# A causal depthwise convolution as Toeplitz products: from two token phases of 64 channels to four token phases of 32 channels

## The chip, the cores and the metric

The kernel runs on one core of one Trainium2 chip. The metric is the device time of one execution in microseconds (us). The engines are named PE (TensorE, matmul), PEld (its weight loads), DVE (VectorE), ACT (ScalarE), POOL (GpSimd) and SP (SyncE, which issues the weight DMAs).

## The reference, cut to what matters

The program is a transformer of two blocks over 512 tokens with 1024 channels, all in float32. The change touches one piece of the first block, the convolution branch of the hybrid mixer:

```python
proj = xn @ w_in                    # 1024 -> 384 + 256 + 32 + 2 * 512
a, gate = jnp.split(conv_in, 2, axis=-1)
c = a * jax.nn.sigmoid(gate)        # 512 tokens x 512 channels
c = causal_depthwise_conv(c, conv_w, conv_b)     # width 31
c = jax.nn.silu(layer_norm(c, conv_ln_g, conv_ln_b))
return jnp.concatenate([attn, c], axis=-1) @ w_o
```

For every channel, the output at token t is the bias plus the sum over k of `conv_w[k]` times the input at token t - 30 + k.

## The kernel before, in words

Channels lie on the 128 partitions and tokens along the free dimension. `project` (L405) is the common matmul: two weight units of 128x1024 for a tile pair, each float32 product split in three (`three`, L399: high by high, high by low, low by high), so that a projection of two tiles is 48 matmuls of 512 columns. A weight unit goes through four slots: SP loads `raw`, ACT rounds it to `WH` (`upper`, L836, a few units ahead of the one in use, when PE has finished with the slot), POOL subtracts to get `WL` (`lower`, L367), and PE waits for POOL's `wlo`. The output tiles of the projections take the PSUM banks 0 to 3 in turn. PE may start a projection only when DVE has emptied the bank that it had four tiles earlier (`tile_free`).

The first block begins with seven input projections (L543 to L547). In the order of execution they give: convolution channels 0 and 1 (in tiles of 128), their gates, channels 2 and 3, their gates, two tiles of the low-rank query, its third tile with the rotary key, and two tiles of the low-rank key/value. DVE works in the order of its code, from L1351: constants (`small`, `taps_of`), then 36 small copies that lay out the taps, biases and a sign (L1356 to L1365), then eight times `lower_h` and `add_square` (input split and sum of squares, L1367), the inverse root (L1404), `channels(0)`, `gates(0)`, `rope_table()`, `channels(2)`, `gates(2)`, `rope_sign()`, `stack` (L1474), `lag_products(0)` and `(1)`, and the low-rank tiles (L1479 on).

The convolution runs on PE as products with Toeplitz matrices. `gates` multiplies channels by the sigmoid of the gates and writes them to `U` by phase (L1452): even and odd tokens of 64 channels go to the two halves of the partitions, so that one group `g` holds 64 channels in two phases and there are GPE = 8 groups. `lag_products(g)` (L1370) makes, in one DVE instruction of 128x2048 elements, the matrices of a group: two stacked identities (`stack`) times the taps (`taps_of`). There are two buffers `tz`. `conv_group(g)` (L458) on PE adds LAGS = 16 products of 256 columns into half a PSUM bank of banks 4 to 7; each float32 product is recorded as two weight loads and two matmuls. `conv_out(g)` (L952) on ACT adds the bias and puts the two phases back in `cacc`, in 2 activations of 64x256.

PE's order is: seven projections, `total(2)` (a sum over partitions for the query's norm), `conv_group(0)`, `total(1)` (for the key/value's norm), `conv_group(1)` to `(7)`, then the query projections (L558). ACT's order is: the squares and roots of the norms, the roundings of `qkv` (L944, L949), all `conv_out` (L962), then the work for the query projections. DVE makes `lag_products(2)` at L1515 between the two parts of the low-rank norms and `(3)` to `(7)` at L1518. The function `convolve` does nothing here (CDV = 0).

Of the kernel before, what the change touches and what calls it, by code (L numbers as in the profile page):

```python
# [8 lines left out]
S, D, P = 512, 1024, 128  # L9
# [3 lines left out]
CC, CW = 512, 31  # L13
CPE = 4
GPE, LAGS = 2 * CPE, 16
# [44 lines left out]
class Mark:  # L60
# [13 lines left out]
    def next(self, k=1):  # L74
        self.n += k
        return self.upto()
# [49 lines left out]
def build(nc, io):  # L126
# [3 lines left out]
    with ExitStack() as ctx:  # L130
# [40 lines left out]
        PADW = S + CW - 1  # L171
        UW = S // 2 + LAGS - 1
        CDV = 4 - CPE
        cpad = cut(0, max(CDV, 1), PADW)
        U = cut(CDV * PADW, GPE, UW)
        lnsq = cut(0, 4, S)
        cacc = cut(2168, 4, S)
        V1 = cut(4216, TT, S)
# [3 lines left out]
        pos, ang, red, whole = cut(6264, S), cut(6776, S), cut(7288, 2, S), cut(8312, 2, S)  # L182
        PT1 = [cut(x, 1280) for x in (6264, 7544)]
        O1 = cut(8824, 2, S)
# [97 lines left out]
        def col(name, c=0):  # L282
            return vec[:, VO[name] + c:VO[name] + c + 1]
# [111 lines left out]
        def _(pe):  # L395
# [157 lines left out]
            for g in range(1, GPE):  # L553
                if g == 3:
                    pe.wait_ge(sems["norm_std"], m["norm_sum"].n)
                conv_group(g)
# [12 lines left out]
            def convolved(c):  # L569
                if c < CDV:  # L570
                    pe.wait_ge(sems["taps"], 1 + CDV * CW)
                else:
                    pe.wait_ge(sems["ce_done"], 4 * (c - CDV + 1))

# [257 lines left out]
        def _(act):  # L832
# [119 lines left out]
            def conv_out(g):  # L952

                act.wait_ge(sems["tz_used"], g + 1)
                ch = 8 - GPE + g
                for f in range(2):
                    nc.scalar.activation(cacc[64 * (ch % 2):64 * (ch % 2) + 64, ch // 2, 1 - f::2],
                                         ps[HALF[f], 4 + g % 4, 256 * (g // 4):256 * (g // 4) + 256], ACT.Identity,
                                         bias=small[HALF[f], BIAS2 + g:BIAS2 + g + 1])\
                      .then_inc(sems["ce_done"], 1)  # L960
# [348 lines left out]
        def _(dve):  # L1309
# [44 lines left out]
            dve.wait_ge(*m["taps"].upto())  # L1354
            dve.wait_ge(sems["prep"], 1)
            for i in range(4):  # L1356
                V.tensor_copy(small[32 * i:32 * i + 32, SIGN:SIGN + 1], vec[96:128, VO["sign"]:VO["sign"] + 1])\
                 .then_inc(sems["prep"], 1)
            for g in range(GPE):
                c, rows = (8 - GPE + g) // 2, HALF[g % 2]  # L1360
                first = VO["conv_w"] + c
                for i in range(2):
                    V.tensor_copy(taps_of[HALF[i], g, 1 - i:CW + 1 - i], vec[rows, first:first + 4 * CW - 3:4]).then_inc(sems["prep"], 1)
                    V.tensor_copy(small[HALF[i], BIAS2 + g:BIAS2 + g + 1], vec[rows, VO["conv_b"] + c:VO["conv_b"] + c + 1])\
                     .then_inc(sems["prep"], 1)  # L1365

            for c in range(DC):  # L1367
                lower_h("g_mix_pre", c)
                add_square(c)
            def lag_products(g):  # L1370

                if g >= 2:
                    dve.wait_ge(sems["tz_used"], g - 1)
                V.tensor_tensor(tz[:, g % 2, :].rearrange("p (e n) -> p e n", n=64),  # L1374
                                stack.unsqueeze(1).to_broadcast([P, 2 * LAGS, 64]),
                                taps_of[:, g, :].unsqueeze(2).to_broadcast([P, 2 * LAGS, 64]), MUL).then_inc(sems["tz_ok"], 1)
# [28 lines left out]
            def taps():  # L1405
                for first in range(0, CDV, 2):
                    for k in range(CW):
                        for c in (first, first + 1):
                            yield k, c

            steps = taps()
            base = m["taps"].n

            def convolve(n):
                for _ in range(n):
                    k, c = next(steps, (None, None))
                    if k is None:
                        return
                    if k:
                        dve.wait_ge(*m["taps"].upto(-1))  # L1420
                    w = vec[:, VO["conv_w"] + 4 * k + c:VO["conv_w"] + 4 * k + c + 1]
                    if k == 0:
                        V.tensor_scalar(cacc[:, c, :], cpad[:, c, 0:S], w, col("conv_b", c), MUL, ADD)\
                         .then_inc(*m["taps"].tick())
                    else:
                        V.scalar_tensor_tensor(cacc[:, c, :], cpad[:, c, k:k + S], w, cacc[:, c, :], MUL, ADD)\
                         .then_inc(*m["taps"].tick())


            def channels(c0):  # L1430
                for j in range(2):
                    c = c0 + j
                    dve.wait_ge(*landed(2, 2, j))
                    V.tensor_tensor(cpad[:, c, CW - 1:PADW] if c < CDV else cacc[:, c, :], bank(j), rstd[:, :], MUL)\
                     .then_inc(*m["tile_free"].tick())
                close(2, 2)

            def gates(c0):
                for j in range(2):
                    dve.wait_ge(*landed(2, 2, j))  # L1440
                    V.tensor_tensor(gt[:, j, :], bank(j), rstd[:, :], MUL).then_inc(*m["tile_free"].tick())
                close(2, 2)
                for j in range(2):
                    c = c0 + j
                    dve.wait_ge(*m["gt_sig"].next())
                    if c < CDV:
                        V.tensor_tensor(cpad[:, c, CW - 1:PADW], cpad[:, c, CW - 1:PADW], gt[:, j, :], MUL)\
                         .then_inc(*m["c_ok"].tick())
                    else:
# [4 lines left out]
                dve.wait_ge(*m["c_ok"].upto())  # L1454
# [12 lines left out]
            gates(0)  # L1467
            rope_table()
            channels(2)
            convolve(6)  # L1470
            gates(2)
            rope_sign()
            dve.wait_ge(sems["ident_in"], 16)
            V.tensor_tensor(stack, ident[:, 0:64], ident[:, 64:128], ADD).then_inc(sems["prep"], 1)  # L1474
            dve.wait_ge(sems["prep"], 6 + 4 * GPE)
            lag_products(0)
            lag_products(1)
            convolve(2)
# [4 lines left out]
            convolve(8)  # L1483
# [13 lines left out]
            convolve(2)  # L1497
# [5 lines left out]
            V.tensor_tensor(HL[:, KRR, :], V1[:, 3, :], HH[:, KRR, :].bitcast(f32), SUB).then_inc(sems["krr_lo"], 1)  # L1503
            invert(V1[:, 0, :])
            add_square(1)
            dve.wait_ge(*m["norm_inv"].upto())
            for c in range(3):
                normalised(c, "g_q_a", c, V1[:, 0, :])
            invert(V1[:, 1, :])
            for c in range(3):  # L1510
                lower(HL[:, c, :], qkv[:, c, :], HH[:, c, :], m["qkv_hi"], m["qkv_lo"])
# [3 lines left out]
            lag_products(2)  # L1515
            for c in range(3, 5):
                lower(HL[:, c, :], qkv[:, c, :], HH[:, c, :], m["qkv_hi"], m["qkv_lo"])
            for g in range(3, GPE):  # L1518
                lag_products(g)
            convolve(18)  # L1520


            for j in range(4):
# [17 lines left out]
                convolve(4)  # L1541
# [6 lines left out]
            convolve(CDV * CW)  # L1548
# [641 lines left out]
```

## Time and profile before

| | |
|---|---|
| Median of 3 runs | 2067.32 us (2065.76 to 2072.4) |
| The profiled execution's own time | 2066.39 us |
| Its span (first to last instruction) | 2064.4 us |
| Mean granted PE clock | 0.959 of full speed |
| PE busy | 1931.6 us, 94% of the span |
| DVE busy | 1039.4 us, 50% |
| ACT busy | 709.2 us, 34% |
| POOL busy | 751.1 us, 36% |

Busy time is the union of an engine's records. A PE record lasts longer than the step from one record to the next, since matmuls are pipelined, so rates are read from the number of records in a stretch. The convolution and what stands around it lie in the first 165 us of the span.

### The profile page before, as it was taken

The numbers are of one execution on the slowest core, as the hardware profiler recorded it, in microseconds if no ns is written. First come the engines' busy times: TensorE is split into PE (matmuls) and PEld (weight loads), VectorE is DVE, ScalarE is ACT, GpSimd is POOL, SyncE is SP. The second block draws the span as 40 slices with busy tenths as digits, with TensorE's granted clock in tenths as the row PEclk, the third lists the DMA queues.
The fourth block names the chain that finished last, engine by engine and source line by source line (L and its number), as shares of the span: only waits on it lengthen the run. The fifth ranks groups of instructions, "written<-read, shape, count | busy, mean of one in ns | idle before, by whom it ended". The sixth has DMA issues, their size and how long they took to land.

```text
span 2064.4 us, 24634 instructions
## 1 busy us (share of the span) xinstructions
PE 1931.6 (94%) x9080; PEld 1558.7 (76%) x9080; DVE 1039.4 (50%) x1648; ACT 709.2 (34%) x1167; POOL 751.1 (36%) x319
## 2 busy tenths in 40 slices
PE   6999885999999789999999999999878899999997
PEld 5877563888888577788888888898755588888885
DVE  7744538734434555344534433740487726333444
ACT  4324633222222333124222222422368833222221
POOL 4302031454354334253535454435200035443541
PEclk9999997999999899999999999997889999999998
DMA  5201021333233222593323333233101122322321
GB/s 168 90 23 62 1 82 31 102 102 95 88 98 106 66 87 90 96 201 122 113 91 95 94 106 103 73 101 105 48 22 32 52 72 88 106 92 91 95 94 56
DMA packets 52233, 177.48 MB, mean 86 GB/s; under 512 B 5527, under 2 KB 5911, under 8 KB 52152
## 3 DMA queue, kind: packets, MB, share of 16 engines
q1 hardware_dynamic: 47952, 166.22, 25.7%
q10 hardware_dynamic: 4200, 10.15, 3.3%
q8 instruction: 55, 0.90, 0.2%
q14 instruction: 26, 0.21, 0.0%
HBM read 166.88 MB, written 9.47 MB: 85 GB/s over the span
## 4 chain that ended last, share of the span: by engine, by line
PE 86%; DVE 9%; ACT 3%; issue 2%; DMA 0%; DVEq 0%; ACTq 0%
PE ps L401 26%; PE ps L403 26%; PE ps L402 26%; PE ps L466 2%; DVE arena L2014 1%; DVE arena L1997 1%; PE ps L804 1%; PE ps L781 1%; DVE acc L1333 1%; PE ps L769 1%; DVE h L1626 1%; PE ps L522 1%; ACT arena L1273 1%; PE ps L455 1%; DVE rstd L1338 0%
## 5 line engine op out<-in xcount | busy, mean ns | idle before, releaser
L370 POOL TENSOR_TENSOR WL<-raw,WH 128x1024 fp32r<-128x1024 f32 x295 | 735.9, 2509 | 1258.0 <-ACT WH L854 1257.9
L401 PE MATMUL ps<-XH,WH 128*128 128x512 f32 (+1 forms) x1280 | 504.9, 394 | 55.4 <-DVE XL L1343 36.7
L402 PE MATMUL ps<-XL,WH 128*128 128x512 f32 (+1 forms) x1280 | 501.1, 391 | 0.0
L403 PE MATMUL ps<-XH,WL 128*128 128x512 f32 (+1 forms) x1280 | 501.0, 391 | 0.0
L854 ACT ACTIVATE WH<-raw 128x1024 fp32r<-128x1024 f32 x295 | 304.0, 1053 | 549.5 <-PE ps L403 510.5
L401 PE MATMUL ps<-HH,WH 128*128 128x512 f32 x1072 | 422.9, 394 | 5.8 <-DVE HL L1727 3.7
L402 PE MATMUL ps<-HL,WH 128*128 128x512 f32 x1072 | 420.0, 392 | 0.0
L403 PE MATMUL ps<-HH,WL 128*128 128x512 f32 x1072 | 419.9, 392 | 0.0
L401 PEld LDWEIGHTS ps<-XH,WH 128*128 128x128 f32 x1280 | 248.5, 194 | 112.8 <-issue 40.4
L403 PEld LDWEIGHTS ps<-XH,WL 128*128 128x128 f32 x1280 | 248.3, 194 | 48.8
L402 PEld LDWEIGHTS ps<-XL,WH 128*128 128x128 f32 x1280 | 248.9, 194 | 47.9 <-issue 0.5
L401 PEld LDWEIGHTS ps<-HH,WH 128*128 128x128 f32 x1072 | 203.3, 190 | 51.2 <-issue 9.2
L402 PEld LDWEIGHTS ps<-HL,WH 128*128 128x128 f32 x1072 | 203.3, 190 | 43.2 <-issue 1.0
L403 PEld LDWEIGHTS ps<-HH,WL 128*128 128x128 f32 x1072 | 202.9, 189 | 42.6
L1840 DVE TENSOR_TENSOR h<-h,ps 128x512 f32<-128x512 f32 x112 | 75.6, 685 | 160.9 <-PE ps L403 160.9
L1348 DVE TENSOR_TENSOR XL<-arena,XH 128x512 fp32r<-128x512 f32 x88 | 134.1, 1563 | 13.6 <-ACT XH L1287 9.9
L1823 DVE SCALAR_TENSOR_TENSOR arena<-ps,rstd 128x512 f32<-128x512 f32 x64 | 44.1, 691 | 181.6 <-PE ps L403 181.0
L1182 ACT ACTIVATE XH<-arena 128x512 fp32r<-128x512 f32 x64 | 40.4, 632 | 256.7 <-DVE arena L1823 256.4
L1273 ACT ACTIVATE arena<-arena,small 128x128 f32<-128x128 f32 (+3 forms) x128 | 70.5, 561 | 7.0 <-DVE small L1997 7.0
L1997 DVE CUSTOM_DVE_ANT_0 arena<-ps,arena 128x128 f32<-128x128 f32 (+3 forms) x128 | 56.2, 487 | 25.1 <-PE ps L769 23.0
L1700 DVE TENSOR_TENSOR arena<-arena,ps 128x512 f32<-128x512 f32 x48 | 33.0, 687 | 70.7 <-PE ps L403 70.5
L466 PE MATMUL ps<-arena 128*128 128x256 f32 x256 | 58.6, 392 | 4.0 <-DVE arena L1374 4.0
(226 smaller groups left out, 1713.2 us busy)
## 6 DMA issues: line engine op xcount, KB each, us to landing
raw<-in_weights SPq DMA_DIRECT2D x301, 512.0 KB, 3.6
tab<-arena ACTq DMA_DIRECT2D x1, 5120.0 KB, 78.5
arena<-tab SPq DMA_DIRECT2D x16, 256.0 KB, 2.9
ftab<-arena ACTq DMA_DIRECT2D x1, 2080.0 KB, 23.7
h<-in_xT SPq DMA_DIRECT2D x8, 256.0 KB, 8.8
out_T<-h SPq DMA_DIRECT2D x8, 256.0 KB, 2.2
arena<-ftab ACTq DMA_DIRECT2D x4, 256.0 KB
arena<-in_pT ACTq DMA_DIRECT2D x1, 512.0 KB, 3.6
```

The costliest lines, as they stand in the source:

```text
L370: nc.gpsimd.tensor_tensor(WL[:, s, :], raw[:, s, :], WH[:, s, :].bitcast(f32), SUB)\
L401: nc.tensor.matmul(out, wh, xh, start=start, stop=False)
L402: nc.tensor.matmul(out, wh, xl, start=False, stop=False)
L403: return nc.tensor.matmul(out, wl, xh, start=False, stop=stop)
L466: last = nc.tensor.matmul(ps[:, 4 + g % 4, 256 * (g // 4):256 * (g // 4) + 256], tz[:, g % 2, at:at + P], U[:, g, LAGS - 1 - k:UW - k], st ...
L854: nc.scalar.activation(WH[:, s, :], raw[:, s, :], ACT.Copy).then_inc(*m["whi"].tick())
L1182: nc.scalar.activation(XH[:, 4 * par + 2 * pr + t, :], rt[:, 2 * pr + t, :], ACT.Square)\
L1273: nc.scalar.activation(a, a, ACT.Exp, bias=small[:, NMX + c:NMX + c + 1], scale=-1.0, accum_out=small[:, SUM + c:SUM + c + 1]).then_inc(se ...
L1348: V.tensor_tensor(out, src, up_.bitcast(f32), SUB).then_inc(*lo.tick())
L1823: V.scalar_tensor_tensor(rt[:, 2 * pr + t, :], bank(t), 0.0, rstd[:, :], MAX, MUL)\
L1840: V.tensor_tensor(h[:, c, :], h[:, c, :], bank(t), ADD).then_inc(*m["tile_free"].tick())
L1997: V.tensor_tensor_reduce(out=job.p(n, r)[:, POFF[qs]:POFF[qs] + w], in0=ps[:, 2 * (c % 2) + r, at:at + w], in1=strips[:, job.heads[r] % 4, ...
```

## The change

The convolution takes four phases instead of two. A group now has 32 channels by 4 phases (PH = 4), there are GPE = 16 groups, LAGS = 9 products of 128 columns each, and four `tz` buffers of 1152 columns instead of two of 2048. `gates` writes `U` in 64 instructions of 32x128 in all instead of 16 of 64x256. `conv_out` is 4 activations of 32x128 per group, 64 in all, instead of 16 of 64x256. PSUM banks 4 to 6 hold one group each; a group waits for the output of the group three before it. The small copies move from the head of DVE's program into `prepare()`, between `gates(0)` and `rope_table()`, with three additions that build `stack` from four identities. `lag_products` 0 to 2 stand before the low-rank tiles, 3 before the first low-rank inverse, 4 and 5 around the second, 6 where 2 stood, and 7 to 15 at the end. A wait of PE before group 3, which had long been met, is gone.

```diff
-        U = cut(CDV * PADW, GPE, UW)
+        U = cut(0, GPE, UW)
...
-        tz = cut(6264, 2, 2048)
-        stack, taps_of = cut(15480, 64), cut(15544, GPE, 32)
+        tz = cut(5744, 4, 32 * TAPS)
+        stack, taps_of = cut(15480, 32), cut(15512, 4, 4 * TAPS)
...
-                if g >= 4:
-                    pe.wait_ge(sems["ce_done"], 2 * (g - 3))
+                if g >= 3:
+                    pe.wait_ge(sems["ce_done"], PH * (g - 2))
                 pe.wait_ge(sems["tz_ok"], g + 1)
-                pe.wait_ge(*m["u_ok"].next(2))
+                pe.wait_ge(*m["u_ok"].next(PH))
                 for k in range(LAGS):
-                    at = 64 * (2 * LAGS - 2 - 2 * k)
-                    last = nc.tensor.matmul(ps[:, 4 + g % 4, 256 * (g // 4):256 * (g // 4) + 256], tz[:, g % 2, at:at + P],
-                                            U[:, g, LAGS - 1 - k:UW - k], start=k == 0, stop=k == LAGS - 1,
-                                            skip_group_check=True)
+                    at = 32 * PH * (LAGS - 1 - k)
+                    last = nc.tensor.matmul(ps[:, 4 + g % 3, 0:P], tz[:, (g + 1) % 4, at:at + P],
+                                            U[:, g, LAGS - 1 - k:UW - k], start=k == 0, stop=k == LAGS - 1)
...
-                for f in range(2):
-                    nc.scalar.activation(cacc[64 * (ch % 2):64 * (ch % 2) + 64, ch // 2, 1 - f::2],
-                                         ps[HALF[f], 4 + g % 4, 256 * (g // 4):256 * (g // 4) + 256], ACT.Identity,
+                c, q = divmod(g, 4)
+                for f in range(PH):
+                    rows = slice(32 * f, 32 * f + 32)
+                    nc.scalar.activation(cacc[32 * q:32 * q + 32, c, PH - 1 - f::PH], ps[rows, 4 + g % 3, 0:P], ACT.Identity,
...
+            def prepare():
+                dve.wait_ge(*m["taps"].upto())
+                dve.wait_ge(sems["prep"], 1)
+                for i in range(PH):
+                    rows = slice(32 * i, 32 * i + 32)
+                    V.tensor_copy(small[rows, SIGN:SIGN + 1], vec[96:128, VO["sign"]:VO["sign"] + 1]).then_inc(sems["prep"], 1)
+                    for q in range(4):
+                        of = slice(32 * q, 32 * q + 32)
+                        V.tensor_copy(taps_of[rows, q, 4 * (PH + 1 - i):4 * (PH + 1 - i + CW)],
+                                      vec[of, VO["conv_w"]:VO["conv_w"] + 4 * CW]).then_inc(sems["prep"], 1)
+                        V.tensor_copy(small[rows, BIAS2 + 4 * q:BIAS2 + 4 * q + 4], vec[of, VO["conv_b"]:VO["conv_b"] + 4])\
+                         .then_inc(sems["prep"], 1)
...
+                V.tensor_tensor(stack, ident[:, 0:32], ident[:, 32:64], ADD).then_inc(sems["prep"], 1)
+                for i in (2, 3):
+                    dve.wait_ge(sems["prep"], 9 * PH + i)
+                    V.tensor_tensor(stack, stack, ident[:, 32 * i:32 * i + 32], ADD).then_inc(sems["prep"], 1)
...
             def lag_products(g):
-                if g >= 2:
-                    dve.wait_ge(sems["tz_used"], g - 1)
+                if g >= 4:
+                    dve.wait_ge(sems["tz_used"], g - 3)
...
-                        for half in range(2):
-                            for f in range(2):
-                                V.tensor_tensor(U[HALF[f], 2 * (c - CDV) + half, LAGS - 1:UW], cacc[HALF[half], c, f::2],
-                                                gt[HALF[half], j, f::2], MUL).then_inc(sems["u_ok"], 1)
+                    for q in range(4):
+                        of = slice(32 * q, 32 * q + 32)
+                        for f in range(PH):
+                            V.tensor_tensor(U[32 * f:32 * f + 32, 4 * c + q, LAGS - 1:UW], cacc[of, c, f::PH], gt[of, j, f::PH], MUL)\
+                             .then_inc(sems["u_ok"], 1)
...
             channels(0)
             gates(0)
+            prepare()
             rope_table()
```

## Rows read from the trace of the kernel before

**Rows 1.** The page: engines' busy time, and the chain that ended last.

```profile
PE 1931.6 (94%) x9080; PEld 1558.7 (76%) x9080; DVE 1039.4 (50%) x1648; ACT 709.2 (34%) x1167; POOL 751.1 (36%) x319
...
PE 86%; DVE 9%; ACT 3%; issue 2%; DMA 0%; DVEq 0%; ACTq 0%
```

**Rows 2.** Busy time by stretch, count in brackets, granted clock after POOL.

```profile
55.00:66.00 11.00, 10.40 (x47) 8.33 (x45) 10.59 (x15) 2.67 (x3) 2.68 (x1) 1.00 0.27 86
88.00:99.00 11.00, 11.00 (x49) 9.01 (x48) 5.18 (x8) 3.76 (x8) 4.39 (x7) 1.00 0.26 81
119.00:124.00 5.00, 5.00 (x13) 4.01 (x12) 2.74 (x2) 0.00 (x0) 0.00 (x0) 0.50 0.00 0
124.00:163.00 39.00, 39.00 (x182) 34.08 (x182) 9.17 (x4) 5.01 (x11) 0.00 (x0) 1.00 0.00 1
```

**Rows 3.** Timeline of PE: the fifth projection, and around the convolution.

```profile
65.93 0.47 PE L401 MATMUL ps<-XH,WH 128*128 128x512 f32 x1 [0.60 <-DVE arena L1434]
...
98.67 1.02 PE L455 MATMUL ps<-acc,ones 128*128 128x512 f32 x2
...
107.30 7.07 PE L466 MATMUL ps<-arena 128*128 128x256 f32 x32
...
118.38 44.49 PE L466 MATMUL ps<-arena 128*128 128x256 f32 x192 [4.01 <-DVE arena L1374]
162.53 0.59 PE L401 MATMUL ps<-HH,WH 128*128 128x512 f32 x1
```

**Rows 4.** Timeline of DVE, the small copies at the head.

```profile
5.11 0.68 DVE L1357 COPY small<-vec 32x1 f32<-32x1 f32 x4 [3.69 <-DMA vec<-in_vecs]
5.83 0.18 DVE L1363 COPY arena<-vec 64x31 f32<-64x31 f32 x1
5.93 0.14 DVE L1364 COPY small<-vec 64x1 f32<-64x1 f32 x1
6.10 0.18 DVE L1363 COPY arena<-vec 64x31 f32<-64x31 f32 x1
...
7.47 2.30 DVE L1363 COPY arena<-vec 64x31 f32<-64x31 f32 x1
...
14.37 0.75 DVE L1343 SCALAR_TENSOR_TENSOR XL<-h,vec,XH 128x512 fp32r<-128x512 f32 x1
```

**Rows 5.** Timelines of POOL and ACT: weight units, and the first input tile.

```profile
7.38 2.35 POOL L370 TENSOR_TENSOR WL<-raw,WH 128x1024 fp32r<-128x1024 f32 x1 [6.29 <-ACT WH L854]
...
45.99 7.48 POOL L370 TENSOR_TENSOR WL<-raw,WH 128x1024 fp32r<-128x1024 f32 x3 [6.85 <-ACT WH L854]
...
83.70 4.77 POOL L370 TENSOR_TENSOR WL<-raw,WH 128x1024 fp32r<-128x1024 f32 x2 [7.50 <-ACT WH L854]
...
7.20 0.71 ACT L896 ACTIVATE XH<-h,vec 128x512 fp32r<-128x512 f32 x1
```

**Rows 6.** The chain of waits in order of time, from `gates(0)` on.

```profile
44.65 0.42 DVE arena L1452
...
45.10 0.42 DVE arena L1452
...
46.01 2.65 DVE arena L1452
...
65.18 0.61 DVE arena L1434
```

**Rows 7.** Timeline of DVE: a product of 64x512, then lag products and a low-rank tile.

```profile
89.65 0.69 DVE L1490 TENSOR_TENSOR arena<-arena 64x512 f32<-64x512 f32 x1
90.37 0.68 DVE L1491 TENSOR_TENSOR arena<-arena 64x512 f32<-64x512 f32 x1
...
76.32 4.50 DVE L1374 TENSOR_TENSOR arena<-arena 128x2048 f32<-128x2048 f32 x2
80.73 1.28 DVE L1458 TENSOR_TENSOR arena<-ps,rstd 128x512 f32<-128x512 f32 x2
```

**Rows 8.** Float32 weight loads and matmuls of 128 columns elsewhere in the program.

```profile
1416.33 0.97 PEld L710 LDWEIGHTS ps<-arena 128*128 128x128 f32 x4
...
235.89 1.31 PE L504 MATMUL ps<-ident,arena 128*128 128x128 f32 x10
...
L710 PEld LDWEIGHTS ps<-arena x4: 333/333/333, 1416.3 to 1417.0; 128*128 128x128 f32 x4
```

**Rows 9.** Timeline of ACT: the last rounding and the first conv outputs.

```profile
115.50 1.29 ACT L949 ACTIVATE HH<-arena 128x512 fp32r<-128x512 f32 x2 [6.10 <-DVE arena L1462]
116.70 2.02 ACT L957 ACTIVATE arena<-ps,small 64x256 f32<-64x256 f32 x4
```

More of the change, by code:

```diff
@@ L13 @@
 CC, CW = 512, 31
-CPE = 4
-GPE, LAGS = 2 * CPE, 16
+PH = 4
+GPE, LAGS = 4 * PH, 9
+TAPS = PH * LAGS
 FC = 22
@@ L168, in cut @@
             return v.rearrange("p (a b) -> p a b", a=shape[0]) if len(shape) == 2 else v
[L171 to L174, printed above, removed]
-        U = cut(CDV * PADW, GPE, UW)
+        UW = S // PH + LAGS - 1
+        U = cut(0, GPE, UW)
         lnsq = cut(0, 4, S)
-        cacc = cut(2168, 4, S)
-        V1 = cut(4216, TT, S)
-        tz = cut(6264, 2, 2048)
-        stack, taps_of = cut(15480, 64), cut(15544, GPE, 32)
+        cacc = cut(2176, 4, S)
+        V1 = cut(4224, TT, S)
+        tz = cut(5744, 4, 32 * TAPS)
+        stack, taps_of = cut(15480, 32), cut(15512, 4, 4 * TAPS)
         SIGN, BIAS2 = 224, 225
-        pos, ang, red, whole = cut(6264, S), cut(6776, S), cut(7288, 2, S), cut(8312, 2, S)
-        PT1 = [cut(x, 1280) for x in (6264, 7544)]
-        O1 = cut(8824, 2, S)
+        pos, ang, red, whole = cut(6272, S), cut(6784, S), cut(7296, 2, S), cut(8320, 2, S)
+        PT1 = [cut(x, 1280) for x in (6272, 7552)]
+        O1 = cut(8832, 2, S)
         mask1 = cut(10360, S)
@@ L569, in convolved @@
             def convolved(c):
[L570 to L573, printed above, removed]
+                pe.wait_ge(sems["ce_done"], 4 * PH * (c + 1))
             ln_total(cacc, convolved, "ln_sum")
@@ L954, in conv_out @@
                 act.wait_ge(sems["tz_used"], g + 1)
-                ch = 8 - GPE + g
-                for f in range(2):
-                    nc.scalar.activation(cacc[64 * (ch % 2):64 * (ch % 2) + 64, ch // 2, 1 - f::2],
-                                         ps[HALF[f], 4 + g % 4, 256 * (g // 4):256 * (g // 4) + 256], ACT.Identity,
-                                         bias=small[HALF[f], BIAS2 + g:BIAS2 + g + 1])\
-                      .then_inc(sems["ce_done"], 1)
+                c, q = divmod(g, 4)
+                for f in range(PH):
+                    rows = slice(32 * f, 32 * f + 32)
+                    nc.scalar.activation(cacc[32 * q:32 * q + 32, c, PH - 1 - f::PH], ps[rows, 4 + g % 3, 0:P], ACT.Identity,
+                                         bias=small[rows, BIAS2 + 4 * q + c:BIAS2 + 4 * q + c + 1]).then_inc(sems["ce_done"], 1)
             for g in range(GPE):
@@ L1353, in _ @@
             dve.wait_ge(sems["vec_in"], 16)
[L1354 to L1365, printed above, removed]
             for c in range(DC):
@@ L1369, in _ @@
                 add_square(c)
-            def lag_products(g):
-                if g >= 2:
-                    dve.wait_ge(sems["tz_used"], g - 1)
-                V.tensor_tensor(tz[:, g % 2, :].rearrange("p (e n) -> p e n", n=64),
-                                stack.unsqueeze(1).to_broadcast([P, 2 * LAGS, 64]),
-                                taps_of[:, g, :].unsqueeze(2).to_broadcast([P, 2 * LAGS, 64]), MUL).then_inc(sems["tz_ok"], 1)
+            def prepare():
[10 more added lines that the diff above has]
+                         .then_inc(sems["prep"], 1)
+                dve.wait_ge(sems["ident_in"], 16)
+                dve.wait_ge(sems["prep"], 1 + 9 * PH)
+                V.tensor_tensor(stack, ident[:, 0:32], ident[:, 32:64], ADD).then_inc(sems["prep"], 1)
+                for i in (2, 3):
+                    dve.wait_ge(sems["prep"], 9 * PH + i)
+                    V.tensor_tensor(stack, stack, ident[:, 32 * i:32 * i + 32], ADD).then_inc(sems["prep"], 1)
+                dve.wait_ge(sems["prep"], 9 * PH + 4)
+            def lag_products(g):
+                if g >= 4:
+                    dve.wait_ge(sems["tz_used"], g - 3)
+                c, q = divmod(g, 4)
+                V.tensor_tensor(tz[:, (g + 1) % 4, :].rearrange("p (e n) -> p e n", n=32),
+                                stack.unsqueeze(1).to_broadcast([P, TAPS, 32]),
+                                taps_of[:, q, c::4].unsqueeze(2).to_broadcast([P, TAPS, 32]), MUL).then_inc(sems["tz_ok"], 1)
             def rope_table():
@@ L1404, in _ @@
             invert(rstd[:, :])
[L1405 to L1427, printed above, removed]
             def channels(c0):
@@ L1433, in channels @@
                     dve.wait_ge(*landed(2, 2, j))
-                    V.tensor_tensor(cpad[:, c, CW - 1:PADW] if c < CDV else cacc[:, c, :], bank(j), rstd[:, :], MUL)\
+                    V.tensor_tensor(cacc[:, c, :], bank(j), rstd[:, :], MUL)\
                      .then_inc(*m["tile_free"].tick())
@@ L1445, in gates @@
                     dve.wait_ge(*m["gt_sig"].next())
[L1446 to L1449, printed above, removed]
-                        for half in range(2):
-                            for f in range(2):
-                                V.tensor_tensor(U[HALF[f], 2 * (c - CDV) + half, LAGS - 1:UW], cacc[HALF[half], c, f::2],
-                                                gt[HALF[half], j, f::2], MUL).then_inc(sems["u_ok"], 1)
-                dve.wait_ge(*m["c_ok"].upto())
+                    for q in range(4):
[3 more added lines that the diff above has]
+                             .then_inc(sems["u_ok"], 1)
             def low_rank(c, j):
@@ L1467, in _ @@
             gates(0)
+            prepare()
             rope_table()
             channels(2)
-            convolve(6)
             gates(2)
             rope_sign()
[L1473 to L1478, printed above, removed]
+            for g in range(3):
+                lag_products(g)
             for j in range(2):
@@ L1482, in _ @@
             close(2, 2)
-            convolve(8)
             low_rank(2, 0)
@@ L1496, in _ @@
             close(2, 2)
-            convolve(2)
             for j in range(2):
@@ L1503, in _ @@
             V.tensor_tensor(HL[:, KRR, :], V1[:, 3, :], HH[:, KRR, :].bitcast(f32), SUB).then_inc(sems["krr_lo"], 1)
+            dve.wait_ge(sems["krr_lo"], 1)
+            lag_products(3)
             invert(V1[:, 0, :])
@@ L1508, in _ @@
                 normalised(c, "g_q_a", c, V1[:, 0, :])
+            lag_products(4)
             invert(V1[:, 1, :])
+            lag_products(5)
             for c in range(3):
@@ L1514, in _ @@
                 normalised(c, "g_kv_a", c - 3, V1[:, 1, :])
-            lag_products(2)
+            lag_products(6)
             for c in range(3, 5):
                 lower(HL[:, c, :], qkv[:, c, :], HH[:, c, :], m["qkv_hi"], m["qkv_lo"])
-            for g in range(3, GPE):
+            for g in range(7, GPE):
                 lag_products(g)
-            convolve(18)
             for j in range(4):
@@ L1540, in _ @@
                 close(1, 2)
-                convolve(4)
             for t in range(4):
@@ L1547, in _ @@
             close(1, 4)
-            convolve(CDV * CW)
             for t in range(4):
```

2 lines of the change are left out of this document (removed).

## The prediction

> **What bounds the kernel now.** I read the page first. PE is busy for 94% of the span, and the chain that ended last is 86% PE [rows 1], so the time is PE's work plus PE's waits. The table by stretch then tells where PE waits around this change. In a stretch of projections (88 to 99 us) PE has no gap [rows 2], and three projections run from 65.93 to 98.67 us, 10.9 us each [rows 3]. Between 55 and 66 us it misses 0.60 us, and the timeline names DVE's `channels(2)` as the releaser: the fifth projection waits for the bank that DVE empties [rows 3]. So DVE sets PE's pace there with nothing to spare, although DVE's share over the whole span is only 50%. From 118.38 us PE runs 192 records of the convolution, six groups, in 44.15 us up to the next projection's first record at 162.53 [rows 3], the first 5.6 us of it at half clock (0.50, against 1.00 after) [rows 2].
>
> All sums are in the profiled execution's own time, 2066.39 us; the median of the runs shown is 0.93 above it. A difference of 0.3%, 6.2 us, is about what a measurement of this kernel can tell from none.
>
> **The convolution on PE.** Before, a record of 256 columns takes (7.07 - 0.38) / 31 = 0.216 us, a group of 32 records 6.91 us [rows 3]. After, a group is 9 products, 18 records of 128 columns. If columns set the pace, a record is 0.108 us. The weights, loaded as often per product, could set it: four float32 loads of the same form step by (0.97 - 0.333) / 3 = 0.212 us at half clock, so 0.106 at full, and ten transposes of 128 columns at full clock take at most (1.31 - 0.27) / 9 = 0.115 us each [rows 8]. Load and stream thus hide each other. I take 0.1095, a group 1.97 us, 16 groups 31.5 against 55.3. The ends for a record are 0.107 and 0.190 (loads that don't overlap at all).
>
> **Not all of those 24 us can be had**, since the new waits put most groups late. ACT reaches `conv_out(0)` only after its last `qkv` rounding, done at 116.79 us [rows 9], and group 3 now needs that output, where before group 4 was the first to need it and stood behind 118.38 anyway. On DVE, `lag_products(3)` and `(5)` now stand on the chain to that rounding. A lag product of 1152 elements takes 2.22 us (4.50 less its own 2.28) less 896 / 0.96 ns, 1.29 us [rows 7]. Of two of them 2.4 us stay (0.2 us goes into a short wait for ACT's root). The rounding ends at 119.2, four outputs at 0.41 us each follow, and group 3 starts at 120.95. 0.41 is the 0.51 between the old 64x256 outputs less 128 elements at the 0.8 ns by which a 1024-element activation outlasts a 512-element one [rows 9]. From there 13 groups by 1.97 are 25.6 us, and PE has stood idle for over 6 us, so I add 2.5 us for half clock (5.6 us at half clock cost 2.8 before [rows 2]; ends 1.5 and 3.4). The next projection starts at 149.05, not 162.53: **-13.5 us**. ACT needs 1.64 us per group and DVE 1.29, both under 1.97, so PE stays the bound.
>
> **The head.** DVE's small copies last from 5.11 to 14.37 us, 9.26 us [rows 4], and `lower_h` waits behind them. They go. In their place DVE waits for the first rounded tile, until 7.91 (7.20 + 0.71) [rows 5]. But two of the copies took 2.2 us more than their like (2.30 against 0.18) [rows 4] exactly while POOL made a weight unit (7.38, 2.35 us) [rows 5]. These two blockings, 4.3 us, now fall on `lower_h`. Gain: 9.26 - 2.8 - 4.3, **-2.2 us**.
>
> A rule bears on this. The Trainium skill, page "SBUF — State Buffer", section on the ports, says that VectorE and GpSimd share one port pair by an exclusive lock for a whole instruction. The trace agrees (2.65 us for a product that else takes 0.42); by a rule of shared bandwidth the head would give back 4.3 us more.
>
> **DVE between `gates(0)` and `channels(2)`.** Products of 64x512 step by 0.72 us [rows 7], those of 64x256 by 0.45 [rows 6], so 128 elements fewer save 0.135 and 64 to 32 partitions save nothing: 0.32 us. `gates(0)` goes from 8 x 0.45 to 32 x 0.32: +6.6 us. `prepare()` has 16 pairs of copies. A pair steps by 0.27 us today [rows 4], with 93 elements more 0.35, so 5.6; four sign copies by 0.17 are 0.7; three additions, each waiting for the one before, some 0.25 each: +7.0 us. POOL's four blockings stay, as the number of its units there (three from 45.99, one later) [rows 5] doesn't change. Together +13.6, less 2.2 from the head: `channels(2)` and with it the fifth projection, which starts at 65.93 [rows 3], start at 77.3. PE finishes the fourth at 63 and stands idle for 14 us, where it had 0.6. Bounds for the copies and products: 0.27 to 0.45 each.
>
> **DVE between `channels(2)` and the seventh projection.** Another +6.6 in `gates(2)`; three lag products of 1.29 for two of 2.24 and the 0.65 us of `stack`: -1.3. The low-rank tiles, at 80.73 [rows 7], move by 11.4 + 5.3. Behind them ACT squares them and only then rounds unit 12, which POOL had ready at 86.1 (83.70 + 2.4) [rows 5], for a projection that began at 87.8 (98.67 less 10.9) [rows 3]. Now it is ready at 102.8. PE, after 77.3 + 21.8 + 2.6 for half clock, is there at 101.7 and waits. So the half clock of the fifth projection costs nothing by itself; what counts is 102.9 for 87.8, +15.0 us, and 0.4 for a clock that may drop once more: **+15.4 us**. This holds the -2.2 of the head.
>
> **Sum:** 15.4 - 13.5 = +1.9 us. Everything behind 162.53 is PE-bound as before and moves with it; POOL's memset, the PSUM banks and the DMAs cost nothing, since their units are ready before PE needs them. 2066.39 + 1.9 + 0.93 = 2069.2 us.
>
> **Rivals.**
> 1. *The gain wins.* Only if DVE's small instructions overlap: the pair 64x31 then 64x1 steps by 0.10 where the outputs stay on the same partitions [rows 4]. If the new products stepped by 0.25 rather than 0.32, each `gates` call would give back 2.2 us and `prepare()` some 2; with the clock at full from group 3 on (2.5) the sum is 1.9 - 2.2 - 2.2 - 2 - 2.5 = -7, 2060. Against it: all these outputs change partitions from one to the next, and such pairs step by 0.17 with one element. Chance 0.19.
> 2. *Slower: the wider stride costs.* `gates` now reads every fourth float, every second before, and ACT writes so. If each element then took two cycles, a product would step by 0.455 rather than 0.32: 64 x 0.135 = 8.6 us on DVE, all on the chain to unit 12. ACT's group would take 4 x 0.51 = 2.04, 0.07 over PE's, 1 us. The sum is +11.5, 2079. It decides from 0.39 us a product on. For it: nothing in the trace reads so at length. Against: copies of 31 such elements outlast copies of one by 0.04 us [rows 4], 1.3 ns an element where 1.04 is a cycle. The Trainium skill, page "SBUF — State Buffer", on cachelines, says that two hits per 16 bytes are needed for full rate; by that rule this is the case. Chance 0.24.
> 3. *Weight loads bind.* A record of 0.190 us makes 13 groups 44.5 us instead of 25.6: +21, 2088. The step at half clock speaks against it [rows 8]. Chance 0.05.
>
> **How the numbers follow.** The forecast, near balance, has 0.52; of it 0.05 falls over +6.2 (products at 0.38 instead of 0.32 alone add 64 x 0.06 = 3.8). So within 0.3%: 0.47; slower: 0.24 + 0.05 + 0.05 = 0.34; faster: 0.19. The forecast's own range is 2062 to 2076. The range that holds 8 in 10 reaches to the first two rivals with their bounds: 2057 to 2082.
>
> **What would show it.** In the profile after: PE idle before the fifth projection, 10 to 17 us, released by DVE's `channels(2)`; a second, short wait of PE for POOL's unit 12; `gates` products at 0.29 us (0.42 would be rival 2); conv records every 0.11 us; group 3 released by ACT's `conv_out`; the query projection 2 us later than 162.5. The forecast is wrong if PE's idle time before the fifth projection is under 7 us, or if groups 4 to 15 take over 2.2 us each.

## The result, and the profile after

The changed kernel takes 2078.36 us (median of 14 runs, 2075.55 to 2086.78), the kernel before 2069.47 (14 runs, 2065.76 to 2072.4). The ratio is 1.0046, 95% interval 1.0035 to 1.0057: some 9 us slower, beyond the 6.2 us that counted as no change. The forecast was 2069.2 us with 0.47 for "within 0.3%" and 0.34 for slower, and a range of 2057 to 2082. The range holds the result. The likeliest case, "within 0.3%", did not come; "slower" did, and the measured change is 8.9 us where +1.9 was summed up.

The page of the changed kernel: busy time, then the chain's shares. PE has 10 us less to do and the span is longer, so PE waits more; DVE's share of the chain is 11% instead of 9% [rows 1].

```profile
PE 1921.3 (92%) x9112; PEld 1550.3 (75%) x9112; DVE 1061.0 (51%) x1706; ACT 732.0 (35%) x1215; POOL 751.1 (36%) x319
...
PE 84%; DVE 11%; ACT 3%; issue 2%; DMA 0%; POOL 0%; DVEq 0%; ACTq 0%
```

The timeline of PE in the changed kernel: the first record after each wait, and the first of the query projection. These answer to [rows 3].

```profile
80.14 0.76 PE L399 MATMUL ps<-XH,WH 128*128 128x512 f32 x1 [16.71 <-DVE arena L1409]
...
109.02 0.79 PE L399 MATMUL ps<-XH,WH 128*128 128x512 f32 x1 [4.52 <-POOL WL L368]
...
143.97 29.23 PE L464 MATMUL ps<-arena 128*128 128x128 f32 x234 [8.85 <-ACT arena L950]
172.96 0.48 PE L399 MATMUL ps<-HH,WH 128*128 128x512 f32 x1
```

All three waits that the prediction named are there, with the releasers it named: DVE's `channels(2)` before the fifth projection (80.14 where it was 65.93), POOL's unit 12 before the seventh (109.02 where it was 87.8), and ACT's first output before group 3. The query projection starts 10.4 us later than before (172.96 against 162.53). PE's list of waits (total us, times, longest) has a fourth one, which the prediction did not name:

```profile
PE ps L453 <- DVE acc L1324: 3.7, 1, 3.7
```

Group 0 is short now (2 us instead of 6.9), so PE reaches `total(1)` before DVE has made its sum, which stands behind `lag_products(3)` and an inverse root. By itself this wait costs nothing in the changed kernel, since group 3 is released later, by ACT. It stays in e1 to e3 and e5 to e8 (3.7 to 4.0 us).

The table by stretch of the changed kernel (columns as in [rows 2]) shows PE at half clock for a while behind each of the three waits. In the first wait the clock fell while PE stood idle; in the second (104 to 109 us) it was still full, and half right behind it.

```profile
66.00:80.00 14.00, 0.00 (x0) 0.00 (x0) 12.97 (x42) 0.58 (x1) 0.00 (x0) 0.57 0.00 0
80.00:85.00 5.00, 4.87 (x12) 3.83 (x13) 4.17 (x9) 4.97 (x10) 0.85 (x1) 0.50 0.01 3
104.00:109.00 5.00, 0.50 (x3) 0.08 (x1) 3.18 (x5) 3.64 (x5) 2.38 (x2) 1.00 0.00 2
109.00:112.00 3.00, 2.98 (x7) 2.40 (x8) 2.97 (x3) 0.00 (x0) 2.75 (x1) 0.50 0.59 172
144.00:150.00 6.00, 6.00 (x28) 6.00 (x29) 1.36 (x1) 5.49 (x12) 0.00 (x0) 0.50 0.00 0
150.00:173.00 23.00, 23.00 (x209) 23.00 (x208) 10.86 (x8) 21.02 (x44) 0.00 (x0) 1.00 0.01 1
```

The timeline of DVE in the changed kernel, answering to [rows 6] and [rows 7]:

```profile
31.50 3.35 DVE L1329 RECIPROCAL rstd<-rstd 128x512 f32<-128x512 f32 x1 [5.57 <-ACT rstd L874]
...
42.31 21.46 DVE L1424 TENSOR_TENSOR arena<-arena 32x128 f32<-32x128 f32 x32
63.80 0.14 DVE L1354 COPY small<-vec 32x1 f32<-32x1 f32 x1
63.97 0.21 DVE L1357 COPY arena<-vec 32x124 f32<-32x124 f32 x1
64.11 0.15 DVE L1359 COPY small<-vec 32x4 f32<-32x4 f32 x1
64.30 0.21 DVE L1357 COPY arena<-vec 32x124 f32<-32x124 f32 x1
...
70.52 0.43 DVE L1383 CAST arena<-arena 128x512 f32<-128x512 int32 x1
...
79.30 1.28 DVE L1409 TENSOR_TENSOR arena<-ps,rstd 128x512 f32<-128x512 f32 x2
...
82.45 16.84 DVE L1424 TENSOR_TENSOR arena<-arena 32x128 f32<-32x128 f32 x32 [0.67 <-ACT arena L904]
...
103.66 1.28 DVE L1429 TENSOR_TENSOR arena<-ps,rstd 128x512 f32<-128x512 f32 x2
```

The timelines of POOL during the first call of `gates`, and of ACT in the outputs of the last 12 groups:

```profile
44.09 7.53 POOL L368 TENSOR_TENSOR WL<-raw,WH 128x1024 fp32r<-128x1024 f32 x3 [6.84 <-ACT WH L846]
53.78 2.41 POOL L368 TENSOR_TENSOR WL<-raw,WH 128x1024 fp32r<-128x1024 f32 x1 [2.16 <-ACT WH L846]
...
151.13 24.50 ACT L950 ACTIVATE arena<-ps,small 32x128 f32<-32x128 f32 x48 [0.91 <-PE ps L464]
```

And the two new forms, by line (durations are minimum, median, maximum in ns):

```profile
L1424 DVE TENSOR_TENSOR arena<-arena x64: 367/378/2490, 42.3 to 98.9; 32x128 f32<-32x128 f32 x64
...
L950 ACT ACTIVATE arena<-ps,small x64: 462/484/497, 141.9 to 175.1; 32x128 f32<-32x128 f32 x64
```

A product of 32x128 lasts 0.378 us, where the prediction looked for 0.29, and steps by 0.41 (the last 17 take 6.89 us), where it had 0.32. An output steps by 0.51 us (24.50 / 48), where it had 0.41. That is the surprise of this profile. Calls of `gates` take 21.5 and 16.8 us, of which 32 x 0.41 = 13.1 is their own. The rest, 8.4 and 3.7 us, falls in POOL's units: the longest product lasts 2.49 us where most last 0.378.

### The profile page after: what moved, and what is told of

Read it like the earlier page. It is cut to its first block, busy times and chain, and to the rows that moved or that the text cites. A ratio compares the mean times of both kernels' runs of the same rounds, so it can differ in the third digit from the quotient of the medians.

```text
span 2079.3 us, 24812 instructions
## 1 busy us (share of the span) xinstructions
PE 1921.3 (92%) x9112; PEld 1550.3 (75%) x9112; DVE 1061.0 (51%) x1706; ACT 732.0 (35%) x1215; POOL 751.1 (36%) x319
## 4 chain that ended last, share of the span: by engine, by line
PE 84%; DVE 11%; ACT 3%; issue 2%; DMA 0%; POOL 0%; DVEq 0%; ACTq 0%
PE ps L399 26%; PE ps L401 25%; PE ps L400 25%; DVE arena L1424 2%; PE ps L464 1%; DVE arena L1980 1%; PE ps L796 1%; DVE arena L1963 1%; PE ps L773 1%; DVE acc L1324 1%; PE ps L761 1%; PE ps L519 1%; DVE h L1592 1%; ACT arena L1264 1%; DVE rstd L1329 0%
## 5 line engine op out<-in xcount | busy, mean ns | idle before, releaser
L400 PEld LDWEIGHTS ps<-HL,WH 128*128 128x128 f32 x1072 | 203.3, 190 | 43.1 <-issue 1.0
L1806 DVE TENSOR_TENSOR h<-h,ps 128x512 f32<-128x512 f32 x112 | 75.5, 684 | 161.0 <-PE ps L401 161.0
L1771 DVE TENSOR_TENSOR h<-h,ps 128x512 f32<-128x512 f32 x32 | 21.8, 683 | 79.9 <-PE ps L401 79.8
```

The source lines that it names most:

```text
L400: nc.tensor.matmul(out, wh, xl, start=False, stop=False)
L1806: V.tensor_tensor(h[:, c, :], h[:, c, :], bank(t), ADD).then_inc(*m["tile_free"].tick())
```

## The experiments

Nine further kernels were run. Most of them move the moment at which the query projection starts, and everything behind that is the same work. The table sets the start of that projection in each profile beside the median of the runs.

| kernel | query projection starts, us | median, us | ratio to before (95%) |
|---|---|---|---|
| before | 162.53 | 2069.47 | 1 |
| changed | 172.96 | 2078.36 | 1.0046 (1.0035 to 1.0057) |
| e1_prod_contig | 163.74 | 2070.60 | 1.0012 (1.0003 to 1.0020) |
| e2_prod_16 | 156.20 | 2061.65 | 0.9973 (0.9962 to 0.9984) |
| e3_prep_gap | 165.94 | 2074.52 | 1.0036 (1.0020 to 1.0052) |
| e4_before_copies_mid | 168.90 | 2072.50 | 1.0026 (1.0015 to 1.0037) |
| e5_outs_contig | 170.52 | 2076.46 | 1.0047 (1.0033 to 1.0062) |
| e6_outs_early | 163.75 | 2071.67 | 1.0016 (1.0007 to 1.0024) |
| e7_dma_u | 156.66 | 2061.15 | 0.9969 (0.9957 to 0.9981) |
| e8_dma_gap_early | 139.92 | 2044.01 | 0.9886 (0.9871 to 0.9900) |
| e9_before_copies_gap | 158.44 | 2065.47 | 0.9983 (0.9973 to 0.9993) |

The difference of the two columns lies between 1903.6 and 1908.6 us in all eleven: what is won or lost ahead of that projection reaches the end, give or take 2.5 us. The kernel before measured 2067.5 to 2069.7 beside the different groups of runs, so the ratios are the better comparison: 0.001 of them is 2.1 us. Of a profile only the part ahead of the query projection is read, since a single execution can differ from the median behind it; the profiled one of e1 took 2083.45 us.

**e1: what the products read.**

```diff
-  cacc[of, c, f::PH], gt[of, j, f::PH], MUL)
+  cacc[of, c, P * f:P * f + P], gt[of, j, P * f:P * f + P], MUL)
```

> The changed kernel, with the 64 products of gates reading 128 consecutive floats instead of every fourth one (the numbers in U are then other tokens' numbers; everything else is done). In the changed kernel such a product lasts 0.378 us and steps by 0.41, where 0.285 and 0.32 were expected. Theory A (the step of 16 bytes slows the reads): duration falls to about 0.285 us, DVE gets 64 x 0.09 = 5.8 us back, all on the chain to the seventh projection, time about 2072.5 (-6). Theory B (a product over 32 partitions has a larger fixed cost, whatever it reads): duration stays 0.37 to 0.38 and the time stays at 2078.

The line of the products in e1:

```profile
L1424 DVE TENSOR_TENSOR arena<-arena x64: 268/283/2457, 41.8 to 92.3; 32x128 f32<-32x128 f32 x64
```

0.283 us, about the 0.29 that the prediction had. Same count, same partitions, as many elements: the 0.095 us come from reading every fourth float. The fifth projection waits 13.7 us instead of 16.7 and the seventh 1.5 instead of 4.5. The time falls by 7.8 us between the medians, by 7.0 between the ratios (1.0012 against 1.0046). Theory A holds; it is the prediction's second rival. The query projection starts 9.2 us earlier, more than the 5.8 of the products: behind a wait of 1.5 us the seventh projection takes 11.9 us and not 13.5, since the clock stays full; 0.6 us comes from the head, which the edit doesn't touch, and 1.0 from a shorter stretch at half clock in the convolution.

**e2: the count of products.**

```diff
-  for q in range(4):
-      of = slice(32 * q, 32 * q + 32)
-      for f in range(PH):
-          V.tensor_tensor(U[32 * f:32 * f + 32, 4 * c + q, ...], cacc[of, c, f::PH], gt[of, j, f::PH], MUL)
+  for q in range(4):
+      V.tensor_tensor(U[:, 4 * c + q, ...], cacc[:, c, q::PH], gt[:, j, q::PH], MUL)
```

> The changed kernel, with 16 products of 128x128 in place of 64 of 32x128 (the phases and channel groups are not moved to their partitions, so U holds wrong channels; PE, ACT and the rest do the same work). Theory A (the count of products is what DVE loses): DVE is relieved of 48 x 0.41 = 19.7 us; the fifth projection starts about 10 us earlier (near 70), the seventh near 94.5, bound by PE again and no longer by unit 12, instead of 109.0; time about 2078.4 - 14.5 = 2064, at or below the kernel before. Rival (the late conv groups and the clock cost as much): the seventh projection moves, but the conv section takes the time back, and the time stays above 2072.

The products' line in e2:

```profile
L1422 DVE TENSOR_TENSOR arena<-arena x16: 379/395/418, 42.3 to 74.2; 128x128 f32<-128x128 f32 x16
```

And eight of them in DVE's timeline of e2:

```profile
42.35 2.49 DVE L1422 TENSOR_TENSOR arena<-arena 128x128 f32<-128x128 f32 x8
```

PE starts the fifth projection at 69.7 us and no longer waits before the seventh; the time is 16.7 us below the changed kernel's by the medians (15.1 by the ratios) and 0.27% below the kernel before. So with most of the products out of the way four phases would beat two. A product over 128 partitions lasts as long as one over 32 (0.395 against 0.378), so the number of partitions is not what made them slow. But eight of them step by (2.49 - 0.39) / 7 = 0.30 us, less than their duration, where the products that change partitions step by 0.41, more than theirs.

**e3 and e4: the small copies and `prepare()`.** In e3 only the call moves:

```diff
             gates(0)
-            prepare()
             rope_table()
...
+            prepare()
             invert(rstd[:, :])
```

> The changed kernel, with prepare() moved from between gates(0) and rope_table() to before the inverse root, where DVE sits idle for 5.6 us. Theory A (prepare is paid in full where it stands): the 6.7 us leave the chain and about 1.1 come back in front, so the fifth and the seventh projection start 5.6 us earlier, time about 2072.8. Rival (what counts is unit 12 and DVE's products behind it, prepare is hidden in PE's wait): under 2 us.

e4 puts the small copies of the kernel before where the change puts `prepare()`, and alters nothing else.

> The kernel before, with nothing changed but its 36 small copies moved from the head of DVE's program to between gates(0) and rope_table(). Theory A (POOL's two blockings fall on the input split instead, so the move gives back only about 2 us in front and costs 5 us in the middle): the fifth projection starts about 3 us later than 65.9, the seventh 2 to 3 us later, time +2 to +3 on the kernel before. Rival (the head gives back all 9.3 us): faster than the kernel before by 1 to 4 us.

PE's waits in e3, from its list of waits (total us, times, longest):

```profile
PE ps L399 <- DVE arena L1410: 10.9, 1, 10.9
...
PE ps L399 <- POOL WL L368: 5.4, 1, 5.4
```

The one wait of PE's that grew in e4, in its timeline:

```profile
69.62 0.77 PE L401 MATMUL ps<-XH,WH 128*128 128x512 f32 x1 [5.82 <-DVE arena L1423]
```

The stretch behind it in e4, in the table by stretch (columns as in [rows 2]):

```profile
69.00:76.00 7.00, 6.38 (x16) 5.05 (x17) 6.17 (x10) 5.67 (x10) 2.36 (x3) 0.53 0.01 2
```

In e3 the query projection starts 7.0 us earlier, somewhat more than the 5.6 expected; the fifth and the seventh start 6.4 earlier. The whole time can't confirm it: the medians differ by 3.8 us and the ratios by 2.1, and the intervals (1.0020 to 1.0052, 1.0035 to 1.0057) overlap. In e4 the fifth projection starts 3.7 us late, about as expected (3), but the time is 0.26% up, 5.4 us (3.1 to 7.7), where 2 to 3 were expected. In the profile the rest is the clock: PE idles for 5.8 us and works at half clock until 75.6 or so (0.53 over 69 to 76), and the delay has grown from 3.7 us to 6.5 at the first `total` (105.18 against 98.67), a further 2.8. I had left that out there, though it stood in the prediction.

**e5: what the outputs write.** `cacc[..., PH - 1 - f::PH]` becomes `cacc[..., P * f:P * f + P]` in `conv_out`.

> The changed kernel, with conv_out writing 128 consecutive floats instead of every fourth one (the tokens of cacc are then permuted). In the changed kernel an output lasts 0.484 us and steps by 0.51, where 0.38 and 0.41 were expected. Theory A (the step of 16 bytes slows ScalarE's writes as it slows DVE's reads): duration about 0.38 us. Theory B (a larger fixed cost of an output over 32 partitions): stays at 0.48. Either way PE's groups, which step by 2.01 us, are PE-bound, so the time moves by under 1 us (2077.5 to 2079).

The outputs by line in e5:

```profile
L950 ACT ACTIVATE arena<-ps,small x64: 342/360/363, 141.4 to 171.9; 32x128 f32<-32x128 f32 x64
```

Two groups of them in ACT's timeline of e5:

```profile
150.70 1.52 ACT L950 ACTIVATE arena<-ps,small 32x128 f32<-32x128 f32 x4 [0.49 <-PE ps L464]
152.71 1.51 ACT L950 ACTIVATE arena<-ps,small 32x128 f32<-32x128 f32 x4 [0.49 <-PE ps L464]
```

The outputs last 0.360 instead of 0.484 us: ACT's writes of every fourth float are slow too. It costs next to nothing here. Groups still step by 2.01 us (150.70 to 152.71), and ACT now idles 0.49 us in each, so PE sets the pace. Only the first four outputs stand in PE's way, 0.5 us. The query projection starts 2.4 us earlier: 0.5 from these outputs, 0.5 from ahead of the convolution, and 1.5 from a shorter stretch at half clock. The time doesn't show it: the ratio is 1.0047, that of the changed kernel.

**e6: the first outputs early.** In ACT's program:

```diff
             close(2, 2)
+            conv_out(0)
             for c in range(3):
...
             root(V1[:, 1, :], KVR)
+            conv_out(1)
+            conv_out(2)
             for c in range(3, 5):
...
-            for g in range(GPE):
+            for g in range(3, GPE):
                 conv_out(g)
```

> The changed kernel, with conv_out(0) placed in ScalarE's program before the roundings of the query part, and conv_out(1) and (2) right behind the second root, before the last two roundings. Theory A (group 3 is late only because ScalarE's first output stands behind the last rounding): group 3 follows group 2 at about 135 us instead of 144, groups 6 and 7 then wait for lag products 6 and 7 (near 143 and 146), the convolution ends near 165.5 instead of 172.9, time about 2071. Rival (PE waits for lag products anyway): under 3 us.

PE's timeline in e6:

```profile
128.60 11.75 PE L464 MATMUL ps<-arena 128*128 128x128 f32 x90
143.29 20.70 PE L464 MATMUL ps<-arena 128*128 128x128 f32 x180 [2.94 <-ACT arena L941]
163.75 0.47 PE L399 MATMUL ps<-HH,WH 128*128 128x512 f32 x1
```

Groups 1 to 5 run in one piece and one wait of 2.9 us is left of 8.85. The projection starts 9.2 us earlier (7.4 expected), since the clock also stays up. The last ten groups step by 2.05 us (20.46 / 10) and not 2.01: here ACT, 4 outputs of 0.51 each, works without a gap from 141.24 on and is the bound, and the slow writes of e5 begin to count.

**e7: 4 products and DMAs.** DVE writes each channel tile phase by phase, and DMAs bring the phases to their partitions through DRAM, on ACT's queue. The edit, cut to what matters:

```diff
-  64 x V.tensor_tensor(U[32 * f:32 * f + 32, 4 * c + q, ...], cacc[of, c, f::PH], gt[of, j, f::PH], MUL)
+  V.tensor_tensor(V1[:, c, :].rearrange("p (f m) -> p f m", f=PH), cacc[:, c, :].rearrange("p (m f) -> p f m", f=PH),
+                  gt[:, j, :].rearrange("p (m f) -> p f m", f=PH), MUL)
...
+  act.dma_start(io["prod"][c * P:(c + 1) * P, :], V1[:, c, :])
...
+  act.dma_start(U[32 * f:32 * f + 32, 8 * pair:8 * pair + 8, LAGS - 1:UW],
+                rows[:, P * f:P * f + P].rearrange("(g p) m -> p g m", p=32))
```

> The changed kernel, computing the same, with the 64 products of 32x128 replaced by 4 of 128x512 that write phase by phase, and DMAs (4 out, 8 back in, through DRAM, on ScalarE's queue) that bring the phases to their partitions. Theory A (the products on DVE are what the change pays with, and a DMA does the move beside other work): gates takes about 2.2 us of DVE instead of 13, the fifth projection starts near 69 instead of 80.1, the seventh is PE-bound near 93.5 instead of 109.0, time about 2063. Rival (the DMAs collide with the weights' or hold ScalarE's queue so that its roundings are late): the seventh projection is late by a weight unit and the time stays over 2068.

The products' line in e7:

```profile
L1440 DVE TENSOR_TENSOR arena<-arena x4: 1073/1093/1132, 42.8 to 73.1; 128x512 f32<-128x512 f32 x4
```

Its DMA issues of these transfers (KB each, us to landing):

```profile
prod<-arena ACTq DMA_DIRECT2D x4, 256.0 KB, 2.0
arena<-prod ACTq DMA_DIRECT2D x8, 128.0 KB, 3.8
```

Four products take 4.4 us of DVE where 64 took 26.2, and the DMAs land within 4 us, tens of us before PE asks. The time is 17.2 us below the changed kernel's by the medians (15.9 by the ratios), ratio to before 0.9969. The products still read every fourth float, 1.09 us each; they are cheaper because each works on all 128 partitions, and few.

**e8: all three.** e7's, e3's and e6's edits together.

> All three edits together: phases moved by DMA, prepare() in DVE's idle stretch before the inverse root, the first three outputs early. If the three costs are separate and stand one behind the other, PE no longer waits before the fifth projection nor before the seventh, the convolution starts near 97 us and ends near 140, and the time is about 2046, below both kernels. Rival (another wait takes their place, so that the sum is less than the parts): over 2055.

PE's timeline in e8:

```profile
96.54 2.17 PE L466 MATMUL ps<-arena 128*128 128x128 f32 x18
102.42 2.07 PE L455 MATMUL ps<-acc,ones 128*128 128x512 f32 x2 [3.71 <-DVE acc L1347]
104.29 10.77 PE L466 MATMUL ps<-arena 128*128 128x128 f32 x90
118.17 22.00 PE L466 MATMUL ps<-arena 128*128 128x128 f32 x180 [3.12 <-ACT arena L960]
139.92 0.48 PE L401 MATMUL ps<-HH,WH 128*128 128x512 f32 x1
```

The waits before the fifth and the seventh projection are gone. The query projection starts 33.0 us before that of the changed kernel; the three edits alone gave 16.3, 7.0 and 9.2, together 32.5. The costs stood one behind the other. The time is 2044.0 us, 0.9886 of the kernel before: it beats both. It doesn't show what four phases are worth by themselves, since two phases with the same DMAs and with early outputs were not tried; only the copies were moved in the kernel before (e9).

**e9: the kernel before, copies in the gap.** As e4, with the copies placed before the inverse root.

> The kernel before, with its 36 small copies moved from the head of DVE's program into DVE's idle stretch before the inverse root (5.1 us there). Theory A (the head gives back about 2 us, as in the changed kernel, and the copies cost nothing in the idle stretch): the first four projections end 1.9 us earlier, DVE keeps its margin of 0.6 us before the fifth, everything behind moves by 1.9, time about 2065.6 (ratio 0.999). Rival (the copies run into the root's way, or DVE cannot follow before the fifth projection): no change or slower.

The ratio is 0.9983 (0.9973 to 0.9993); 0.999 was expected and lies inside. PE starts the fifth projection at 62.92 instead of 65.93, with 0.61 us of waiting as before. That is 3.0 us where 1.9 was expected, and the query projection starts 4.1 earlier: six groups behind PE's wait of 4.0 us take 43.1 us instead of 44.2. So the head's gain is real and was not bound to the four phases.

## Why the prediction was right or wrong

**The head, -2.2.** Right: the inverse root starts at 31.50 where it started at 33.40, 1.9 us earlier. POOL's blockings did fall on `lower_h` and `add_square` instead: four there now (from 8.42, 11.88, 14.64 and 21.20 us), each some 2.1 us, where before two of the four fell on the copies. And e4 shows that the move alone doesn't pay.

**The size of a product: the step that failed.** "128 elements fewer save 0.135 and 64 to 32 partitions save nothing: 0.32 us." That partitions save nothing was right (e2); the elements were not read the same way. From 64x256 to 32x128 the step of the reads went from 8 to 16 bytes, and the product stepped by 0.41. 64 x 0.09 is 5.8 us, half before the fifth and half before the seventh projection, all in PE's waits. In e1, with products as short as forecast, the query projection starts at 163.74, and 164.4 was forecast (162.53 + 1.9). The second rival had the mechanism at 0.24 and a product of 0.455; what it named as its sign, 0.39 a step, was passed. That its 2079 lies next to the measured 2078.4 is partly luck: it had 8.6 us for the products, where they cost 5.8, and 1 us for ACT, where e5 shows at most 0.5; the half clock behind the longer waits made up for part of it. I argued against it from copies of 31 elements and 1.3 ns an element where 1.04 is a cycle. That was a third of the effect and should have counted for it. The Trainium skill, page "SBUF — State Buffer", section "Specifications (TRN2)", asks for two hits in a line of 16 bytes for full bandwidth. This case agrees: at a step of 8 bytes a product of 256 elements takes 0.425 us, on the line between 0.283 for 128 and 0.69 for 512 in a row ([rows 7], e1), and at 16 bytes it takes longer than that line. The products of the kernel before, by line (ns, minimum, median, maximum):

```profile
L1452 DVE TENSOR_TENSOR arena<-arena x16: 408/425/2653, 44.2 to 73.3; 64x256 f32<-64x256 f32 x16
```

**`prepare()`, +7.0.** It took 6.7 (63.80 to 70.52). Right. Behind the head, POOL's four blockings stayed, too: 8.4 us in `gates(0)` now, where before some 6.4 fell there and 2.1 behind it, on a cast of `rope_table()`.

**The fifth projection.** 77.3 expected, 80.14 measured; the 2.8 us are 32 products by 0.09.

**Unit 12.** The mechanism was right and decided the size: PE's seventh projection waits for POOL, whose unit waits behind ACT's squares and DVE's low-rank tiles. The start moved by 21.2 us, not 15.0: 5.8 from the products; the other 0.4 is within the sum's rounding. The projection then ran 3 us at half clock (1.7 lost, not 0.4). The wait was 4.5 us, not 1.2. This is the same error again: in e1 the wait is 1.5 us and nothing is lost behind it.

**The convolution, -13.5.** From the first record of group 0 to the query projection it took 63.0 us before (99.53 to 162.53) and 50.5 after (122.47 to 172.96): -12.5. Group 3 was released by ACT at 21.5 us behind group 0, where 21.4 were expected. Groups step by 2.01 instead of 1.97, 0.5 us over 13, and the half clock lasted 6.0 us and cost 3.0, not 2.5. The fourth wait, at `total(1)`, was not foreseen and cost nothing. That weight loads don't bind was right; the 0.190 us of the third rival had no row behind it. That ACT needs less than PE was right only in its conclusion: 2.04 us per group and not 1.64, behind PE by the end but not in its way after group 3, as e5 shows.

**The sum.** +22.9 ahead of the convolution (15.4 expected) and -12.5 in it (-13.5 expected) give +10.4 in the profiles, +8.9 in the medians. Of the 8.5 us by which this misses +1.9, 5.8 are the products themselves and 1.3 the clock in the seventh projection, which both come from one mis-sized term. The two signs that were to prove the forecast wrong (idle under 7 us, groups over 2.2 us) did not look at that term and stayed silent; the sign named for the second rival, a product of 0.42 instead of 0.29, came out in between, at 0.378. The profiled execution's span is 14.9 us longer; the other 4.5 lie behind the query projection, where PE was busy 4.6 us longer with the same work at a lower granted clock in some stretches. The medians don't have them.

## What to carry to other kernels

Halving an instruction's elements does not halve its time, and doubling the phases doubles the step of its reads: price a new form by its step in bytes as well as by its size. An engine at half load can still be the bound of a stretch; count what it must do between two things that the busy engine waits for, and place preparations in its idle stretches rather than on that path. Where work exists only to move data between partitions, a DMA with time to spare can be the cheaper mover (e7).

## What the runs showed of the hardware

- DVE, products of two float32 operands from SBUF: 0.283 us for 128 elements in a row and 0.378 at a step of four floats (e1), 1.09 us for 512 at that step (e7) against 0.69 in a row [rows 7]. That is 0.74 to 0.78 ns more per element. At a step of two floats no such cost shows: 256 elements in 0.425 us, where the line between 0.283 and 0.69 gives 0.42. Which of the two operands causes it was not tried.
- ACT, writes at a step of four floats: 0.484 us against 0.360 for 128 elements (e5), 0.97 ns per element.
- DVE steps by 0.30 us through products of 0.39 that stay on all partitions (e2), and by 0.41 through products of 0.378 whose output moves to other partitions each time. The copies of `prepare()` show that a move of the input is enough: 32x124 then 32x4 on the same partitions step by 0.14 us where the first lasts 0.21, and the next copy, with the same output partitions and other input partitions, comes 0.19 us later where the one ahead lasts 0.15.
- Between the fifth projection and the query projection, idle stretches of PE of 3.7 to 17 us were each followed by some 3 to 6 us at 1.2 GHz (granted clock 0.50), one of 1.5 us (e1) by none. Behind the one of 5.8 us in e4 a further 2.8 us were lost.
